# One channel tile of a causal convolution moved from VectorE to GpSimd, in a fused decoder step

## The reference

```
h = rmsnorm(x)
a, gate, q, k, v = split(h @ w_in)                  # conv 512 + 512, attention 3 x 512
u = a * sigmoid(gate)
c = causal_depthwise_conv(u, w[31, 512]) + b        # each channel by itself, 31 taps back in time
c = silu(layernorm(c))
q, k = rmsnorm per head(q), rmsnorm per head(k)
o = stick_breaking_attention(q, k, v)
x += concat(c, o) @ w_out ;  x += swiglu(rmsnorm(x))
```

## Time and profile before

| | us |
|---|---|
| median of three runs | 1824.4 |
| the three runs | 1823.2, 1824.4, 1824.5 |
| the profiled execution, its own time | 1818.44 |
| its span | 1816.9 |
| TensorE matmul busy | 1680.1 |
| VectorE busy | 1293.1 |
| ScalarE busy | 1048.5 |
| GpSimd busy | 71.2 |

### The profile page before, as it was taken

The page is one execution under the profiler, slowest core; times in us unless marked ns, Lnnn a source line. Parts: engine busy times, 40 slices in busy tenths (PEclk is TensorE's granted clock), DMA queues, the critical chain, the costliest instruction groups (busy, mean ns, idle before and its releaser), DMA issues.

```text
span 1816.9 us, 24269 instructions
## 1 busy us (share of the span) xinstructions
PE 1680.1 (92%) x9295; PEld 1448.1 (80%) x9295; DVE 1293.1 (71%) x1091; ACT 1048.5 (58%) x913; POOL 71.2 (4%) x94
## 2 busy tenths in 40 slices
PE   4986989998999977939999999999999999999995
PEld 3964989998999876928878878878788788787884
DVE  3796355544965255447888888888888888888885
ACT  3534244434343255227787687777877877877772
POOL 2014000000001000010000000000000000000001
PEclk9998699999999699969999999999999999999998
DMA  6525049756567222638999999999999999999992
GB/s 233 192 70 165 1 153 360 241 174 205 167 204 248 96 79 79 242 132 290 372 350 386 372 357 393 357 370 376 351 389 366 358 392 358 366 378 359 381 368 97
DMA packets 236654, 491.71 MB, mean 271 GB/s; under 512 B 8666, under 2 KB 66138, under 8 KB 236329
## 3 DMA queue, kind: packets, MB, share of 16 engines
q1 hardware_dynamic: 227088, 456.60, 70.1%
q0 software_dynamic: 9504, 34.24, 5.7%
HBM read 463.87 MB, written 27.42 MB: 270 GB/s over the span
## 4 chain that ended last, share of the span: by engine, by line
issue 57%; PE 30%; DVE 8%; ACT 3%; DMA 1%; POOL 0%; POOLq 0%; SPq 0%; ACTq 0%; DVEq 0%
PE bank L611 8%; PE bank L612 7%; PE bank L613 7%; PE bank L897 2%; PE bank L834 1%; DVE even_CA L1521 1%; DVE WL L1462 1%; ACT WH L1138 1%; PE bank L731 1%; DVE RS L1536 1%; DMA R<-in_param 1%; DVE RS L1707 1%; PE bank L885 1%; PE bank L871 0%; POOL moe_rows_in L591 0%
## 5 line engine op out<-in xcount | busy, mean ns | idle before, releaser
L1823 DVE TENSOR_TENSOR WL<-moe_MORE,WH 128x2048 fp32r<-128x2048 f32 x192 | 439.2, 2291 | 86.8 <-ACT WH L1390 86.3
L1390 ACT ACTIVATE WH<-moe_MORE 128x2048 fp32r<-128x2048 f32 x192 | 368.4, 1923 | 150.1 <-PE bank L613 150.0
L1823 DVE TENSOR_TENSOR WL<-ring,WH 128x2048 fp32r<-128x2048 f32 x144 | 329.2, 2291 | 56.8 <-ACT WH L1390 55.4
L611 PE MATMUL bank<-WH,moe_XEH 128*128 128x512 f32 x896 | 360.5, 402 | 3.0 <-DVE moe_XEL L1829 2.3
L613 PE MATMUL bank<-WH,moe_XEL 128*128 128x512 f32 x896 | 354.7, 396 | 0.0
L612 PE MATMUL bank<-WL,moe_XEH 128*128 128x512 f32 x896 | 354.5, 396 | 0.0
L1390 ACT ACTIVATE WH<-ring 128x2048 fp32r<-128x2048 f32 x144 | 275.9, 1918 | 85.4 <-PE bank L613 85.4
L1462 DVE TENSOR_TENSOR WL<-ring,WH 128x2048 fp32r<-128x2048 f32 x80 | 181.0, 2263 | 177.0 <-ACT WH L1138 176.8
L611 PE MATMUL bank<-HH,WH 128*128 128x264 f32 x960 | 283.1, 295 | 19.3 <-DVE HL L1480 18.2
L612 PE MATMUL bank<-HL,WH 128*128 128x264 f32 x960 | 278.2, 290 | 0.0
L613 PE MATMUL bank<-HH,WL 128*128 128x264 f32 x960 | 277.9, 289 | 0.0
(11 more groups left out here) (296 smaller groups left out, 1856.9 us busy)
## 6 DMA issues: line engine op xcount, KB each, us to landing
moe_MORE<-in_moe_w_gate SPq DMA_DIRECT2D x72, 1024.0 KB, 5.9
moe_MORE<-in_moe_w_up SPq DMA_DIRECT2D x72, 1024.0 KB, 6.3
ring<-in_moe_w_down SPq DMA_DIRECT2D x64, 1024.0 KB, 6.5
moe_MORE<-in_moe_w_down SPq DMA_DIRECT2D x48, 1024.0 KB, 5.9
ring<-in_moe_w_gate SPq DMA_DIRECT2D x40, 1024.0 KB, 5.5
ring<-in_moe_w_up SPq DMA_DIRECT2D x40, 1024.0 KB, 6.1
ring<-in_w_in_odd SPq DMA_DIRECT2D x24, 1024.0 KB, 5.4
ring<-in_ffn_w_gate SPq DMA_DIRECT2D x11, 1024.0 KB, 8.1
```

The source lines that it names most:

```text
L611: mm(out, lh, rh, start=start, stop=False)
L1390: func(WH[:, q % WRING, :], chunk(q), ACT.Copy).then_inc(s_hi, 1)
L1823: V.tensor_tensor(WL[:, q % WRING, :], chunk(q), full(WH[:, q % WRING, :]), ALU.subtract)\
```

## The change

The prompt's tile 3 is made on GpSimd, tile 2 stays on VectorE. For each tap GpSimd makes a product (the first straight into the tile, the others into one of two scratch rows of `QN`), and for each tap after the first a sum: 31 products and 30 sums, each sum waiting for its product. They stand on GpSimd's queue after the first two groups of diagonal matrices and before the third. VectorE's taps of tile 2 now each wait for the one just before. The bias of tile 3 is added by a new VectorE instruction ahead of the head norms, which waits for GpSimd's last sum. To free a semaphore, TensorE's count for the cache's transposes is kept in `s_turn`, with the later waits on it raised by four.

```
-            for g in range(2 * CGT):
+            def conv_tile(c):
+
+                pool.wait_ge(s_u, CT)
+                pool.wait_ge(s_zero, 1)
+                acc = CA[:, c, 0:SEQ]
+                for w in range(W):
+                    tap = cw[:, c * W + w:c * W + w + 1].to_broadcast([P, SEQ])
+                    out = acc if w == 0 else QN[:, w % 2, 0:SEQ]
+                    nc.gpsimd.tensor_tensor(out, U[:, c, w:w + SEQ], tap, ALU.mult).then_inc(s_tap, 1)
+                    if w >= 1:
+                        pool.wait_ge(s_tap, 2 * w)
+                        nc.gpsimd.tensor_tensor(acc, acc, QN[:, w % 2, 0:SEQ], ALU.add).then_inc(s_tap, 1)
+
+            spread_taps(0)
+            spread_taps(1)
+            conv_tile(CT - 1)
+            for g in range(2, 2 * CGT):
                 spread_taps(g)
...
-                last.then_inc(s_cct, 1)
+                last.then_inc(s_turn, 1)
...
-                act.wait_ge(s_cct, c + 1)
+                act.wait_ge(s_turn, DK + c + 1)
...
-                for c in (2, 3):
+                for c in (2,):
...
-                        dve.wait_ge(s_dch, before + 2 * (w - 1) + c - 1)
+                        dve.wait_ge(s_dch, before + w)
...
-            steps[0] = before + 2 * W
+            steps[0] = before + W
...
             link(last)
+            dve.wait_ge(s_tap, 2 * W - 1)
+            link(V.tensor_scalar(CA[:, CT - 1, 0:SEQ], CA[:, CT - 1, 0:SEQ], cb[:, CT - 1:CT], None, ALU.add))
             for n in range(2 * HP):
...
-                dve.wait_ge(s_turn, DK + i + 1)
+                dve.wait_ge(s_turn, DK + CT + i + 1)
```

More of the change, by code:

```diff
@@ L273, in build @@
         s_ht = sem("s_ht"); s_hh = sem("s_hh"); s_hl = sem("s_hl")
-        s_zero = sem("s_zero"); s_cct = sem("s_cct"); s_win = sem("s_win")
+        s_zero = sem("s_zero"); s_tap = sem("s_tap"); s_win = sem("s_win")
         s_ag = sem("s_ag"); s_sig = sem("s_sig"); s_u = sem("s_u"); s_ut = sem("s_ut"); s_uo = sem("s_uo")
```

## The result

The changed kernel takes 1845.66 us (median of four runs, 1842.85 to 1846.6) against 1823.8 for the kernel before (four runs, 1820.74 to 1824.5): 1.0121 times the time, interval [1.0103, 1.0138]. That is 21.9 us slower (18.8 to 25.2 by the interval) where 16.8 were forecast, and inside the range. One execution of one experiment took 2849 us at a mean granted clock of 0.618 instead of 0.94, and its run's ratio leaves it out.

A forecast was written before the change was run, and what follows sets the result against it. The prediction took the chain of waits on VectorE up to the head norms as the bound. GpSimd's last sum at 124.9 made the norms 16.8 us later; added to the 1824.4 median this gave 1841.2, range 1830 to 1855.

The forecast's parts named there:

- Bound and cover: VectorE alone carries the chain from 67.62 to 128.2 us; nothing absorbs a head norm shift, which reaches the end whole.
- GpSimd's sum: GpSimd's tile: start at 64.2, 35.4 of instructions, 2.4 of waits, 15.4 and 7.5 of holds; last sum at 124.9.
- Its own part: GpSimd's tile undisturbed: 61 instructions at 0.58 us and 30 waits of 0.08, 37.8 in all, done at 102.0.
- The holds: Time VectorE's two-SBUF-input instructions block GpSimd: seven splits 15.4 us, 30 taps and four sample instructions 7.5 at 0.22 each.
- By the letter of the Trainium skill: Shared ports locked for whole instructions: 34 short holds of 0.47, 16.0 us instead of 7.5, end 8.5 later, about 1850.
- VectorE and the tail: VectorE done at 115.3, waits 9.6 us; after GpSimd's last sum, first head norm product at 129.3, 16.8 later than before.
- so this costs 0 to 1.3; I take 0: TensorE's lower clock in the convolution group forecast for 133.3: perhaps 1.5 us more, 0.27 spare, taken as 0.
- the floor for an earlier start: Head norms cannot start before the first square root at about 104.6; VectorE gains at most 4.3 us there.
- rival 1: Faster: engines do not block each other over short instructions, first product 5.6 us earlier, 1818.8; chance 0.04.
- case 2: No difference: short instructions slip into each other's fixed parts, GpSimd done at 108 to 112, 1821 to 1828; chance 0.06.
- Case 3: GpSimd never lets the shared ports go; VectorE stands from 64.2 to 102.0, norms 26.3 us late, 1850.7; chance 0.13.

The follow-up runs named there:

- plain delay: Kernel before with nine reciprocals that nothing reads added on VectorE ahead of the head norms; 1838.5 us, 1.0097 of the time before.
- run without second inputs: Changed kernel with seven weight splits and the 30 taps of tile 2 as one-input reductions, their results not computed; 1819.7 us, 0.9987 of the time before.
- one tap: Changed kernel with only the first of GpSimd's 31 taps, the other 30 of tile 3 not computed; 1828.4 us, 1.0019 of the time before.
- wait behind the norms: Changed kernel with VectorE's wait for GpSimd and the bias moved after the eight head norms; 1833.65 us, 1.0065 of the time before.
- wait behind the norms, blocks in the tile: Changed kernel with VectorE's wait and bias after the head norms, and GpSimd's third and fourth diagonal block inside its tile after tap 22; 1.0078 of the time before.
- changed kernel, five idle matmuls: Changed kernel with five matmuls that nothing reads on TensorE ahead of the key transposes; 1841.7 us, 1.0104 of the time before.
- changed kernel, eleven idle matmuls: Changed kernel with eleven matmuls that nothing reads on TensorE ahead of the key transposes; 1838.5 us, 1.0085 of the time before.
- before with idle matmuls: Kernel before with four matmuls that nothing reads on TensorE ahead of the key transposes; 1824.6 us, 1.0009 of the time before.
- before with matmuls in the value product: Kernel before with an unread reduced-precision matmul after every second matmul of the samples' value product, 32 in all; 1830.8 us, 1.0038 of the time before.
- one-input splits: Changed kernel with the stretch's seven weight splits as one-input reductions, those low parts not computed; 1829.4 us, 1.0038 of the time before.
- one tap, eight idle matmuls: Changed kernel with only GpSimd's first tap and eight unread matmuls on TensorE ahead of the key transposes; 1824.1 us, 0.9997 of the time before.

## Why the prediction was right, and where its sum was off

**Bound and cover.** That the head norms carry to the end whole was right: the plain delay moved them by 15.3, the stage by 15.6 and the total by 12.8 to 22.6. SyncE's pause ended later by as much as the stage.

**GpSimd's sum** came out at 60.26 (64.82 to 125.08) where 60.7 stood, by two errors that cancel. Its own part was put at 37.8 and is 41.7 (0.6 and 30 pairs of 1.37): the sum of two full tensors takes 0.72, not the 0.58 read from L519. The holds were put at 22.9 and are 18.6. The seven splits hold 13.3, not 15.4: six times 2.67 - 0.80, and 2.84 - 0.72. That leaves 5.3 instead of 7.5 for taps and samples: a pair that meets two taps takes 1.64 (71.27 to 72.91) instead of 1.37, 0.13 a tap and not 0.22. By the letter of the Trainium skill (SBUF — State Buffer, § Who interferes with whom) each would have held for its whole 0.47 and, by the prediction's sum, GpSimd ended at 133.4; the row at 124.36 ends at 125.08. What the same section states about an instruction with at most one SBUF input outside the 2-port modes, that it does not contend, the run without second inputs shows for reductions: 0.61 and 0.73 beside VectorE's.

**VectorE and the tail** were right: its own part done at 116.1 (115.3 forecast), a wait of 9.1 (9.6), GpSimd's third block ahead of the bias (1.90), the first product at 129.45 (129.4). The last agreement holds some luck: this execution reached its gated input 0.6 later, and counted from there the norms moved by 16.3, not 16.8.

**The step that was mis-sized** is "so this costs 0 to 1.3; I take 0", the clock. The convolution group that it looked at did not get slower but faster in the profiled execution (4.76 against 5.91); TensorE then finished sooner and stood 2.66 us ahead of the key transposes, and the clock fell in the work behind that: 4.7 us. With it the 16.8 become 21.5, and 21.9 were measured. The prediction priced the clock where it was low before, and not where it was high and could fall. How often an execution of the changed kernel has this fall is not shown; the interval of the total, 18.8 to 25.2, leaves 2.5 to 8.9 for all that the 16.3 do not explain.

**One step was wrong and did not matter**: the floor for an earlier start was put at the first square root, 4.3 us, and is the splits' own pace, 2.4. With the last norm only 2.2 earlier, rival 1 would have been about 1822 at best, and not 1818.8.

**The rivals.** Case 1 and case 2 (no blocking, or slipping between) fall with the rows of 0.80 and 2.67; and with nothing left in the loop that blocks, the time is that of the kernel before (0.9987 [0.9971, 1.0003]). Case 3 (GpSimd holds on) falls too: VectorE's taps come between GpSimd's instructions from the start, five in 4.24.

## What to carry to other kernels

Before work goes to a second engine, look in the trace for a place where the two already overlap and compare the longest duration of an instruction with its median: one such row (1.79 against 0.49) told that VectorE and GpSimd would take turns, not share. An instruction sequence that is shorter by half is worth only what its other pace leaves, here the splits'. And when a stage moves, price the clock of what follows it as well as its start, and look at more than one execution before giving that price to the change.

## What was not expected of the hardware

TensorE's clock at the key transposes in the profiled executions, with the time it stood just ahead, the duration of the convolution's third group (the shorter it is, the earlier the clock had risen; with one tap it had not fallen ahead of the group), and of the six 512-column matmuls:

| run | third group | stood | six matmuls | clock |
|---|---|---|---|---|
| plain delay | 6.18 | 1.27 | 2.84 | 1.00 |
| no second inputs | 6.13 | 1.30 | 2.84 | 1.00 |
| wait behind the norms | 6.05 | 1.27 | 2.84 | 1.00 |
| before | 5.91 | 1.51 | 2.84 | 1.00 |
| wait behind the norms, blocks in the tile | 5.82 | 1.62 | 2.84 | 1.00 |
| changed kernel, five idle matmuls | 5.73 | filled | 2.84 | 1.00 |
| changed kernel, eleven idle matmuls | 5.67 | filled | 2.84 | 1.00 |
| before with idle matmuls | 5.36 | 0.28 | 2.84 | fell just behind them, next group 4.99 |
| before with matmuls in the value product | 5.24 | 2.19 | 2.84 | fell just behind them, next group 4.75 |
| one-input splits | 5.00 | 2.43 | 5.49 | 0.50 |
| changed kernel | 4.76 | 2.66 | 5.48 | 0.60, then 0.50 |
| one tap, eight idle matmuls | 4.66 | filled | 2.84 | 1.00 |
| one tap | 3.62 | 4.16 | 5.48 | 0.50 |

The kernel before and its run with matmuls in the value product execute the same instructions up to here, and so do the changed kernel and its two runs with idle matmuls up to the idle matmuls; their third groups still differ, so part of what the table shows belongs to the execution and not to the kernel. The seven runs with the longest third group kept the clock, and of the six others only the one with one tap and idle matmuls did. A longer stand goes with a fall too, but the kernel before with idle matmuls lost the clock behind a stand of 0.28, so the stand alone does not explain it. What else sets it stays open. The mean clock of a whole execution of the kernel before goes with its span: 0.951 with 1816.8 us, 0.943 with 1823.9, so some of the spread between executions of one kernel is the clock's; which stage has it was not tried.
